# Latent attention: four modulation steps first, down projection in quarter pieces, softmax two heads deep, other modulation steps spread over the heads

## The chip, the core and the metric

One core of one Trainium2 chip runs the whole program. The metric is the device time of one launch in microseconds. The kernel before takes 2475.97 us (median of 3 runs, 2472.95 to 2480.49).

The core has TensorE (PE: matrix products out of SBUF into PSUM, which has 8 banks here), VectorE (DVE), ScalarE (ACT), GpSimd (POOL) and SyncE (SP), whose queue issues nearly all weight DMAs. Each engine works through its own program in order and waits on semaphores that the others raise.

## What is computed

Two stacks of layers in float32, on 256 tokens of width 1024. The change is in the first layer's mixer, latent attention over 256 latent and 256 context tokens; behind it follow a mixture of experts, a convolution layer, another mixture of experts, and the second stack.

```python
mod_l = (silu(c) @ w_mod[i] + b_mod[i])          # 6 * 1024 columns; mod_c the same of c_ctx
sh1, sc1, g1, sh2, sc2, g2 = split(mod_l, 6)
a_lat = rmsnorm(x, g) * (1 + sc1) + sh1          # a_ctx with the context's
...
ckv = a @ w_dkv                                  # 256 columns and 64 of a rotary key
c_kv = rmsnorm(ckv[..., :256], g_kv);  k_pe = rope(ckv[..., 256:])
k_nope, v = split((c_kv @ w_ukv).reshape(n, 8, 256))
q = (rmsnorm(a_lat @ w_dq, g_q) @ w_uq).reshape(n, 8, 192)   # 128, and 64 with rope
s = q @ concat([k_nope, k_pe]).T * scale         # 256 x 512 a head
o = softmax(s) @ v                               # 8 heads
x = x + g1 * (o @ w_o)
```

## The kernel before

`Mla` computes the latent attention; each of its methods `sync`, `tensor`, `scalar`, `vector`, `gpsimd` is one engine's program, in the order written. Everything is held with channels on the partitions.

Weights come through a ring of six slots of 128 x 4096 floats (2 MB). `Chunk.fetch` (L253) issues the DMA on SP once the slot is free; at the program's start "free" is the landing of all constants (L231). A chunk whose products run in the short float32 form takes two slots: `round_scalar` (L283) rounds the weights on ScalarE into a high part, `rest_vector` (L291) forms the low part on VectorE, and a product is then three passes, high x high, high x low, low x high (`product3`, L566). `round_piece_scalar` and `rest_piece_vector` (L298, L309) do the same for a quarter of the columns and were there already for other stages. A slot is given back by a count that TensorE raises at its last use.

The modulation has 12 steps in this layer (`Modulation`, L345), each over one 2 MB chunk of w_mod: 8 narrow products (L366), a ScalarE copy to a row (L390), four transposes on TensorE (L378, in the helper at L564), a VectorE sum (L397). Steps 0 to 3 give shift and scale for the input, the other 8 are wanted only at the attention's end and later.

Order before. SP fetches steps 0 to 2, w_dq, step 3, w_dkv, steps 4 and 5, the two w_uq, step 6, w_ukv, steps 7 to 11, the two w_o (L798 to L813), and behind it the 12 chunks of the next layer's modulation and the expert weights, the latter as half slots (L339). TensorE: mean of squares, steps 0 to 3, cq (L823, in L606 to L612, `first_linear3_tensor`), ckv and the rotary key in three tiles of 512 columns (L829, in L576), mean of cq, step 4, mean of ckv, step 5, the query products w_uq (L856, in L560) with the rotations, step 6, V (L872), then the heads.

A head h: `scores(h)` makes the keys' own part (bank "kn", L879), VectorE copies it to KN (L1065), four products give the scores in two banks (L892, L893), VectorE takes the maxima (L1072), ScalarE the exponentials with their sums (L983), VectorE divides (L1079). `values(h)` transposes the probabilities (L902), ScalarE copies them to PT (L991), four products with V give o (L908), VectorE splits it in high and low (L1084, L1086). In TensorE's order `scores(h + 1)` stands ahead of a modulation step and `values(h)`; in VectorE's order `values(h)` stands ahead of `softmax(h + 1)`. There is one pair of buffers S and one PT.

PSUM banks are handed out in turn (`Banks.next`, L203): a request waits until the bank's last reader is done; `hold` takes one out of the turn.

## Time and profile before

| | us |
|---|---|
| median of 3 runs | 2475.97 |
| span of the profiled execution | 2478.1 |
| PE busy, share of the span | 2246.1, 91% |
| DVE busy | 1011.6, 41% |
| ACT busy | 744.2, 30% |
| DMA, mean over the span | 249 GB/s |

The page's slices are 62 us each. In the first five PE's tenths are 4, 8, 8, 7, 8, from the sixth on mostly 9. The DMA rate in the first eight is 286, 257, 68, 67, 298, 412, 421, 421 GB/s: the weights of the heads were all fetched early, and the stream comes back with the output projection. The latent attention takes the first 282 us, the first mixture of experts follows.

A float32 product is recorded as two pieces, one of the short form as one. Times of the rows are read from one profiled execution; the clock that the page grants TensorE is told as a share of 2.4 GHz.

### The profile page before, as it was taken

Reading aid. Unit: us, or ns where it says so; the run is one execution under the profiler, and the core shown is the slowest. Engines: PE = TensorE matmul, PEld = TensorE weight load, DVE = VectorE, ACT = ScalarE, POOL = GpSimd, SP = SyncE. Lnnn points to the kernel's source line nnn. Section 1 sums busy time; section 2 is a strip of 40 time slices with the busy share of each in tenths; the row PEclk is TensorE's granted clock in tenths of the full one; section 3 lists DMA queues with packets and bytes.
Section 4 is the critical chain, followed back from the end, with each engine's and each line's share of the span. In section 5 each row is a group of like instructions: output and inputs, shape, how many; then the busy total and the mean of one; then the engine's idle time right before and its main releaser. Section 6 shows DMA issues by size and latency. Waiting matters only on the chain.

```text
span 2478.1 us, 31723 instructions
## 1 busy us (share of the span) xinstructions
PE 2246.1 (91%) x13638; PEld 1500.3 (61%) x13638; DVE 1011.6 (41%) x1735; ACT 744.2 (30%) x1116; POOL 244.3 (10%) x220
## 2 busy tenths in 40 slices
PE   4887899999999797999999997998999889768998
PEld 2633634444444396344444445976899889658988
DVE  2322421111111254211111115875589565546982
ACT  3122311111111242111111114865455343225542
POOL 0000000000000000000000000046136100001540
PEclk8999999999999898999999998999999989889999
DMA  8711899999999445899999984432345444203642
GB/s 286 257 68 67 298 412 421 421 421 421 413 400 401 159 169 205 323 401 399 401 398 401 403 327 139 153 120 68 128 156 177 170 155 170 102 1 104 196 161 85
DMA packets 197490, 616.89 MB, mean 249 GB/s; under 512 B 19936, under 2 KB 82528, under 8 KB 147936
## 3 DMA queue, kind: packets, MB, share of 16 engines
q1 hardware_dynamic: 189376, 610.83, 64.5%
q10 hardware_dynamic: 7968, 3.94, 0.5%
q8 instruction: 112, 1.84, 0.3%
q14 instruction: 34, 0.28, 0.0%
HBM read 613.69 MB, written 1.05 MB: 248 GB/s over the span
## 4 chain that ended last, share of the span: by engine, by line
PE 79%; DVE 9%; ACT 6%; DMA 3%; issue 1%; POOL 1%; SPq 0%; ACTq 0%; DVEq 0%; POOLq 0%
PE bank L576 25%; PE bank L1227 17%; PE bank L1236 9%; PE bank L564 5%; PE bank L1251 5%; PE bank L1200 4%; DVE ring_rounded L294 2%; ACT ring_rounded L288 2%; PE bank L560 2%; DMA ring<-in_w_mod 1%; PE bank L2868 1%; PE bank L366 1%; DMA ring<-in_moe_w_up 1%; DVE rstd L644 1%; PE bank L606 1%
## 5 line engine op out<-in xcount | busy, mean ns | idle before, releaser
L1227 PE MATMUL bank<-ring,arena 128*64 128x512 f32 x2048 | 450.6, 592 | 1.8 <-DVE arena L1586 1.6
L576 PE MATMUL bank<-normed_rounded,ring_rounded 128*128 128x256 f32 (+1 forms) x3368 | 413.2, 285 | 7.2 <-ACT normed_rounded L665 5.7
L576 PEld LDWEIGHTS bank<-normed_rounded,ring_rounded 128*128 128x128 f32 x3368 | 408.1, 190 | 9.5 <-issue 6.5
L294 DVE TENSOR_TENSOR ring_rounded<-ring,ring_rounded 128x4096 fp32r<-128x4096 f32 x69 | 307.8, 4466 | 157.3 <-ACT ring_rounded L288 157.1
L576 PE MATMUL bank<-arena_rounded,ring_rounded 128*128 128x256 f32 (+1 forms) x2416 | 313.6, 290 | 18.1 <-ACT ring_rounded L288 6.0
L1227 PEld LDWEIGHTS bank<-ring,arena 128*64 128x64 f32 x2048 | 147.5, 137 | 293.1 <-issue 291.1
L576 PEld LDWEIGHTS bank<-arena_rounded,ring_rounded 128*128 128x128 f32 x2416 | 301.5, 194 | 28.3 <-DVE ring_rounded L294 6.8
L1591 DVE TENSOR_TENSOR arena<-arena,bank 64x512 f32<-64x512 f32 x64 | 43.5, 680 | 579.4 <-ACT arena L1423 579.4
L288 ACT ACTIVATE ring_rounded<-ring 128x4096 fp32r<-128x4096 f32 x69 | 245.1, 3555 | 73.4 <-DMA ring<-in_ffn_w_down 51.1
L1236 PE MATMUL bank<-ring,arena 128*64 128x512 f32 x1024 | 233.8, 598 | 0.0
L564 PEld LDWEIGHTS bank<-mats,arena 128*128 128x128 f32 (+1 forms) x934 | 121.4, 183 | 110.1 <-issue 83.5
L564 PE MATMUL bank<-mats,arena 128*128 128x128 f32 (+1 forms) x934 | 159.4, 301 | 17.1 <-POOL arena L2346 5.3
L1423 ACT ACTIVATE arena<-bank 64x512 f32<-64x512 f32 x64 | 38.0, 594 | 406.1 <-PE bank L1227 406.1
L1437 ACT ACTIVATE arena<-bank 128x512 f32<-128x512 f32 x64 | 38.2, 597 | 366.9 <-PE bank L1236 366.9
L1236 PEld LDWEIGHTS bank<-ring,arena 128*64 128x64 f32 x1024 | 67.8, 136 | 130.5 <-issue 130.2
L1251 PE MATMUL bank<-arena 64*128 64x256 f32 x1024 | 128.3, 388 | 1.4 <-ACT arena L1437 1.4
L1580 DVE COPY arena<-bank 128x256 f32<-128x256 f32 x64 | 27.2, 425 | 248.0 <-PE bank L1251 242.8
L1200 PE MATMUL bank<-arena 128*64 128x512 f32 x512 | 122.6, 600 | 1.0 <-DVE arena L1554 1.0
L1251 PEld LDWEIGHTS bank<-arena 64*128 64x128 f32 x1024 | 93.7, 185 | 19.3 <-ACT arena L1437 3.2
L2700 DVE SCALAR_TENSOR_TENSOR arena<-arena,cols 128x256 f32<-128x256 f32 x176 | 95.3, 542 | 6.3
L2724 POOL TENSOR_TENSOR arena_rounded<-arena,arena_rounded 128x256 fp32r<-128x256 f32 x44 | 89.4, 2031 | 23.3 <-ACT arena_rounded L2649 23.3
L1200 PEld LDWEIGHTS bank<-arena 128*64 128x64 f32 x512 | 37.2, 138 | 73.6 <-issue 73.6
(257 smaller groups left out, 2103.5 us busy)
## 6 DMA issues: line engine op xcount, KB each, us to landing
ring<-in_moe_w_gate SPq DMA_DIRECT2D x128, 1024.0 KB, 8.9
ring<-in_moe_w_up SPq DMA_DIRECT2D x128, 1024.0 KB, 11.0
ring<-in_moe_w_down SPq DMA_DIRECT2D x128, 1024.0 KB, 8.1
ring<-in_w_mod SPq DMA_DIRECT2D x24, 2048.0 KB, 13.4
ring<-in_ffn_w_up SPq DMA_DIRECT2D x44, 1024.0 KB, 6.7
ring<-in_ssm_w_in SPq DMA_DIRECT2D x12, 2048.0 KB, 8.0
ring<-in_ffn_w_down SPq DMA_DIRECT2D x10, 2048.0 KB, 7.9
ring<-in_conv_w_in SPq DMA_DIRECT2D x6, 2048.0 KB, 9.2
```

The costliest lines, as they stand in the source:

```text
L288: e.activation(ring.rounded[(self.number + 1) % RING][:, 0:n].bitcast(F32R), ring.slots[self.number % RING][:, 0:n], ACT.Copy).then_inc(*s ...
L294: e.tensor_tensor(ring.rounded[slot][:, 0:n].bitcast(F32R), ring.slots[slot][:, 0:n], ring.rounded[(self.number + 1) % RING][:, 0:n], ALU. ...
L560: end = e.matmul(out, lhs(k), rhs(k), start=k == 0, stop=k == n_k - 1)
L564: return e.transpose(out, in_, self.mats[0:rows, 0, 0:rows])
L576: end = e.matmul(out, lhs.bitcast(F32R), rhs.bitcast(F32R), start=start and n == 0 and k == 0, stop=stop and n == 2 and k == n_k - 1)
L1200: end = e.matmul(bank[n * cap:(n + 1) * cap, :], self.mine[x][:, t, :], self.f[:, t, n * 512:(n + 1) * 512], start=t == 0, stop=t == self. ...
L1227: ends[i] = e.matmul(bank[rows, :], self.xt[x][:, j, n * cap:(n + 1) * cap], weights[:, j, :], start=n == 0 and j == 0, stop=n == 1 and j ...
L1236: end = e.matmul(bank[n * cap:(n + 1) * cap, :], self.ht[x][:, k, :], weights[:, i, n * 512:(n + 1) * 512], start=k == 0, stop=k == KF - 1)
L1251: end = e.matmul(self.acc(kk), self.y[x][rows, i * P:(i + 1) * P], self.back[x][rows, :], start=False, stop=last and kk % 2 == 1)
L1591: e.tensor_tensor(h, h, banks.of(key, "h", x)[0:cap, :], ALU.mult).then_inc(*dve.up(key, "h", x))
L2700: e.scalar_tensor_tensor(buf, self.PB[:, s, j, q:q + T], w3[:, q:q + 1], buf, ALU.mult, ALU.add).then_inc(*dve.up())
L2724: e.tensor_tensor(self.H_low[:, m, :].bitcast(F32R), self.H[:, m, :], self.H_high[:, m, :], ALU.subtract).then_inc(*pool.up(key, "h low", m))
```

## The change

Ring: slots that were never used need no wait, so SP issues the first weights without the constants. SP's order is modulation steps 0 to 3, w_dq, w_dkv, both w_uq, steps 4 and 5, w_ukv, steps 6 to 11, w_o.

Down projections: w_dq is rounded in four quarters, each with two tiles of the modulated input of the latent tokens, and TensorE takes them quarter by quarter; the context's half of the input is modulated afterwards. ckv and rotary key are computed for latent and context columns apart, in three banks that are held, with the mean of cq between the two. The query products wait only for the scaled cq; the mean of ckv and the rotations are put between them, steps 4 and 5 behind the two chunks.

Heads: two pairs of S, two PT and `small` for two heads. TensorE's iteration h is the keys of h + 2, the scores of h + 1, a modulation step (6 to 10 in iterations 0 to 4, 11 in iteration 6), the transposes of h, the values of h - 1. ScalarE's is the exponentials of h + 1, the step's row, the PT copies of h; w_o's two chunks are rounded behind those of heads 6 and 7. VectorE's is the sum of an earlier step, o of h - 2, the key copy of h + 2, maxima and division of h + 1; in the last iteration w_o 0's rest is first.

```diff
@@ -228,8 +228,13 @@
...
-        self.number, self.half, self.freed = 0, 0, [(self.k.constants, ("constants",))] * RING
+        self.number, self.half, self.freed = 0, 0, [None] * RING
         self.halves = {}
+
+    def wait_for(self, w, freed):
+        if freed:
+            signal, key = freed
+            w.wait_ge(*signal.at(*key))
 
     def close_halves(self):
...
@@ -254,8 +259,7 @@
...
-        signal, key = ring.freed[slot]
-        w.wait_ge(*signal.at(*key))
+        ring.wait_for(w, ring.freed[slot])
...
@@ -594,13 +596,17 @@
...
 
         pe, (high, low) = self.pe, weights
-        w.wait_ge(*chunk.ready()[0])
-        w.wait_ge(*chunk.ready()[1])
+        if not pieces:
+            w.wait_ge(*chunk.ready()[0])
+            w.wait_ge(*chunk.ready()[1])
         for i in range(n_k):
+            if pieces:
+                w.wait_ge(*self.act.at("high", chunk.name, i * 4 // n_k))
+                w.wait_ge(*self.dve.at("low", chunk.name, i * 4 // n_k))
...
@@ -752,24 +758,24 @@
...
-        self.S = [ar.take(BANK) for _ in range(2)]
+        self.S = [[ar.take(BANK) for _ in range(2)] for _ in range(2)]
...
-        self.KN, self.PT = ar.take(2, T), ar.take(4, SEQ)
+        self.KN, self.PT = ar.take(2, T), [ar.take(4, SEQ) for _ in range(2)]
...
-        self.rest = Modulation(k, 0, 4, 8, lambda at: (early if at < 7 else late)[at % 2])
+        self.rest = Modulation(k, 0, 4, 8, lambda at: (early if at < 6 else late)[at % 2])
...
@@ -796,21 +802,22 @@
...
     def sync(self, e, w):
-        for at in range(3):
+        for at in range(4):
             self.first.fetch(e, w, at)
-        self.w_dq.fetch(e, w)
-        self.first.fetch(e, w, 3)
-        self.w_dkv.fetch(e, w)
-        self.rest.fetch(e, w, 4)
-        self.rest.fetch(e, w, 5)
-        for chunk in self.w_uq:
+        for chunk in (self.w_dq, self.w_dkv, *self.w_uq):
             chunk.fetch(e, w)
-        self.rest.fetch(e, w, 6)
+        for at in (4, 5):
+            self.rest.fetch(e, w, at)
         self.w_ukv.fetch(e, w)
-        for at in range(7, 12):
+        for at in range(6, 12):
             self.rest.fetch(e, w, at)
         for chunk in self.w_o:
             chunk.fetch(e, w)
+
+    step_of = {0: 6, 1: 7, 2: 8, 3: 9, 4: 10, 6: 11}
...
@@ -820,23 +827,29 @@
...
+        def x_ready(c):
+            return lambda part, i: dve.at("mla x", "low", i, c) if part else act.at("mla x", "high", i, c)
+
+        k.first_tiles_tensor(e, w, self.w_dq, "cq", 4, self.q_parts, KD, SEQ, lambda m: dve, x_ready(0), pieces=True)
...
         for m in range(3):
-            which, cols = (0, slice(m * P, (m + 1) * P)) if m < 2 else (1, slice(0, P))
-            bank, emptied = banks.next(dve if m < 2 else act, "ckv", m)
+            _, emptied = banks.next(dve if m < 2 else act, "ckv", m)
+            banks.hold("ckv", m)
             w.wait_ge(*emptied)
-            ends = k.product3(e, w, bank[:, :], [lambda i, v=v: v[which][:, i, cols] for v in (high, low)], self.x_parts, KD,
-                              self.w_dkv.ready())
-            if m == 2:
-                ends[1].then_inc(*pe.up("free", self.w_dkv.number + 1))
-            ends[2].then_inc(*pe.up("ckv", m))
+        for c in range(2):
+            cols = self.cols_of(c)
+            for m in range(3):
+                which, at = (0, slice(m * P, (m + 1) * P)) if m < 2 else (1, slice(0, P))
+                ends = k.product3(e, w, banks.of("ckv", m)[:, cols], [lambda i, v=v: v[which][:, i, at] for v in (high, low)],
+                                  [lambda i, x=x: x(i)[:, cols] for x in self.x_parts], KD, self.w_dkv.ready(), x_ready(c))
+                if c and m == 2:
+                    ends[1].then_inc(*pe.up("free", self.w_dkv.number + 1))
+                if c:
+                    ends[2].then_inc(*pe.up("ckv", m))
+                    banks.drop("ckv", m)
+            if c == 0:
+                k.mean_tensor(e, w, "cq", self.QN, 4, SEQ, 512)
         pe.mark("free", self.w_dkv.number)
...
-        k.mean_tensor(e, w, "cq", self.QN, 4, SEQ, 512)
-        self.rest.step_tensor(e, w, 4)
-        k.mean_tensor(e, w, "ckv", self.squared, 2, T, 256)
-        self.rest.step_tensor(e, w, 5)
...
@@ -845,26 +858,33 @@
...
         for c, chunk in enumerate(self.w_uq):
...
-                w.wait_ge(*dve.at("scaled", "ckv"))
...
+                w.wait_ge(*dve.at("scaled", "cq"))
                 end = k.product(e, bank[:, 0:SEQ], lambda i: weights[:, i, t * P:(t + 1) * P], lambda i: self.CQ[:, i, :], 4)
                 end.then_inc(*pe.up("uq", c, t))
-                if t >= 4:
-                    rotate((c, t), self.QR[:, 2 * c + t - 4, :], act.at("uq", c, t))
+                if (c, t) == (0, 1):
+                    k.mean_tensor(e, w, "ckv", self.squared, 2, T, 256)
+                if (c, t) == (0, 3):
+                    rotate("k", self.raw, act.at("ckv", 2))
+                if t == 5:
+                    rotate_query(c, 4)
+                if (c, t) == (1, 0):
+                    rotate_query(0, 5)
             pe.mark("free", chunk.number)
-        w.wait_ge(*dve.at("turned", (1, 5)))
-        w.wait_ge(*act.at("uq", 1, 5))
-        self.rest.step_tensor(e, w, 6)
+            self.rest.step_tensor(e, w, 4 + c)
...
+        w.wait_ge(*dve.at("scaled", "ckv"))
...
+                if (t, n) == (0, 0):
+                    rotate_query(1, 5)
+
+        def keys(h):
...
+        def scores(h):
             kn = self.KN[:, h % 2, :]
-            outs = []
+            w.wait_ge(*dve.at("turned", (1, 5)))
             for q in range(2):
                 out, emptied = banks.next(act, "exp", h, q)
-                banks.hold("exp", h, q)
                 w.wait_ge(*emptied)
-                outs.append(out)
-            w.wait_ge(*dve.at("kn", h))
-            for q, out in enumerate(outs):
+                w.wait_ge(*dve.at("kn", h))
                 e.matmul(out[:, :], self.QN[:, h, q * P:(q + 1) * P], kn, start=True, stop=False)
                 e.matmul(out[:, :], self.QR[:, h // 2, q * P:(q + 1) * P], self.KPE[:, h % 2, :], start=False, stop=True
                          ).then_inc(*pe.up("scores", h, q))
...
-        def values(h):
+        def turns(h):
...
-                    end = k.turn(e, bank[:, i * P:(i + 1) * P], self.S[q][:, i * P:(i + 1) * P])
+                    end = k.turn(e, bank[:, i * P:(i + 1) * P], self.S[h % 2][q][:, i * P:(i + 1) * P])
...
+        def values(h):
...
             w.wait_ge(*act.at("pt", h, 1))
...
+        keys(0)
+        keys(1)
         scores(0)
         for h in range(MLA_HEADS):
-            for q in range(2):
-                banks.drop("exp", h, q)
+            if h + 2 < MLA_HEADS:
+                keys(h + 2)
             if h + 1 < MLA_HEADS:
                 scores(h + 1)
-            if h < 5:
-                self.rest.step_tensor(e, w, 7 + h, turn=True)
-            values(h)
-        self.rest.close_tensor(e, w)
+            if h in self.step_of:
+                self.rest.step_tensor(e, w, self.step_of[h])
+            turns(h)
+            if h == MLA_HEADS - 1:
+                self.rest.close_tensor(e, w)
+            if h:
+                values(h - 1)
+        values(MLA_HEADS - 1)
...
@@ -940,70 +970,81 @@
...
-        for at in range(3):
+        for at in range(4):
             self.first.step_scalar(e, w, at)
-        self.w_dq.round_scalar(e, w)
-        self.first.step_scalar(e, w, 3)
         w.wait_ge(*dve.at("mod", 0, 0))
-        k.modulated_parts_scalar(e, w, "mla x", 0, T, self.x_parts[0])
+
+        def high(i, c):
+            cols = self.cols_of(c)
...
+            e.activation(self.x_parts[0](i)[:, cols].bitcast(F32R), k.A[:, i, cols], ACT.Identity,
+                         bias=k.mod[:, 0, i, c:c + 1]).then_inc(*act.up("mla x", "high", i, c))
+        for q in range(4):
+            self.w_dq.round_piece_scalar(e, w, q)
+            for i in (2 * q, 2 * q + 1):
+                high(i, 0)
         self.w_dkv.round_scalar(e, w)
+        for i in range(KD):
+            high(i, 1)
+        for i in range(4):
+            w.wait_ge(*dve.at("cq", i))
+            e.activation(self.QN[:, i, :], self.CQ[:, i, :], ACT.Square).then_inc(*act.up("square", "cq", i))
+        k.root_scalar(e, w, "cq", SEQ)
...
+            w.wait_ge(*dve.at("ckv", i))
+            e.activation(self.squared[:, i, :], self.CKV[:, i, :], ACT.Square).then_inc(*act.up("square", "ckv", i))
...
         e.activation(self.raw, banks.of("ckv", 2)[:, :], ACT.Copy).then_inc(*act.up("ckv", 2))
...
-            e.activation(self.squared[:, i, :], self.CKV[:, i, :], ACT.Square).then_inc(*act.up("square", "ckv", i))
...
+        query(0, 0)
+        query(0, 1)
         k.root_scalar(e, w, "ckv", T, dve.at("scaled", "cq"))
-        self.rest.step_scalar(e, w, 5)
-        w.wait_ge(*pe.at("sums", "cq"))
...
         for c in range(2):
-            for t in range(6):
...
-        self.rest.step_scalar(e, w, 6)
+            for t in range(2 if c == 0 else 0, 6):
+                query(c, t)
+            self.rest.step_scalar(e, w, 4 + c)
...
+        exps(0)
         for h in range(MLA_HEADS):
-            if h < 5:
-                self.rest.step_scalar(e, w, 7 + h)
-            if h == MLA_HEADS - 1:
-                self.w_o[0].round_scalar(e, w)
-            values(h)
             if h + 1 < MLA_HEADS:
-                softmax(h + 1)
+                exps(h + 1)
+            if h in self.step_of:
+                self.rest.step_scalar(e, w, self.step_of[h])
+            turned(h)
+            if h >= MLA_HEADS - 2:
+                self.w_o[h - MLA_HEADS + 2].round_scalar(e, w)
         w.wait_ge(*pe.at("mod turn", 0, 11))
-        self.w_o[1].round_scalar(e, w)
...
@@ -1013,30 +1054,50 @@
...
-        for at in range(3):
+        for at in range(4):
...
-        self.w_dq.rest_vector(e, w)
-        self.first.step_vector(e, w, 3)
...
-        k.modulated_parts_vector(e, w, "mla x", 0, T, *self.x_parts)
...
+        for q in range(4):
+            for i in (2 * q, 2 * q + 1):
+                value(i, 0)
+            self.w_dq.rest_piece_vector(e, w, q)
+        for i in range(KD):
+            lower(i, 0)
         self.w_dkv.rest_vector(e, w)
+        for i in range(KD):
+            value(i, 1)
         for m in range(4):
             w.wait_ge(*pe.at("cq", m))
             e.tensor_copy(self.CQ[:, m, :], banks.of("cq", m)[:, 0:SEQ]).then_inc(*dve.up("cq", m))
-        for m in range(2):
-            w.wait_ge(*pe.at("ckv", m))
-            e.tensor_copy(self.CKV[:, m, :], banks.of("ckv", m)[:, :]).then_inc(*dve.up("ckv", m))
-        for buf, n_k, n, name, gain in ((self.CQ, 4, SEQ, "cq", "g_q"), (self.CKV, 2, T, "ckv", "g_kv")):
+        for i in range(KD):
+            lower(i, 1)
+
+        def scaled(buf, n_k, n, name, gain):
             k.root_vector(e, w, name, n)
...
-            if name == "ckv":
-                self.rest.step_vector(e, w, 4)
+        scaled(self.CQ, 4, SEQ, "cq", "g_q")
+        for m in range(2):
+            w.wait_ge(*pe.at("ckv", m))
+            e.tensor_copy(self.CKV[:, m, :], banks.of("ckv", m)[:, :]).then_inc(*dve.up("ckv", m))
+        scaled(self.CKV, 2, T, "ckv", "g_kv")
...
@@ -1087,21 +1150,25 @@
...
-        self.rest.step_vector(e, w, 5)
+        last = MLA_HEADS - 1
         key_part(0)
+        key_part(1)
         softmax(0)
         for h in range(MLA_HEADS):
-            if h + 1 < MLA_HEADS:
-                key_part(h + 1)
-            if h < 5:
-                self.rest.step_vector(e, w, 6 + h)
-            if h == MLA_HEADS - 1:
+            if h == last:
                 self.w_o[0].rest_vector(e, w)
-            values(h)
+            if h in (1, 2, 3, 4, 5, 7):
+                self.rest.step_vector(e, w, 4 + h if h < 6 else 10)
+            if 2 <= h:
+                values(h - 2)
+            if h + 2 < MLA_HEADS:
+                key_part(h + 2)
             if h + 1 < MLA_HEADS:
                 softmax(h + 1)
         self.rest.step_vector(e, w, 11)
         self.rest.close_vector(e, w)
+        values(last - 1)
+        values(last)
         self.w_o[1].rest_vector(e, w)
         for m in range(KD):
```

## Rows read from the trace of the kernel before

**Rows 1.** Chain that ended last, first 150 us: start us, length us, what.
```profile
11.68 0.37 SPq L264
...
47.64 4.33 DVE ring_rounded L294
52.54 6.43 DVE normed L682 x16
...
68.60 16.80 PE bank L576 x72
...
99.19 10.51 PE bank L560 x40
...
113.89 8.65 PE bank L560 x40
...
130.59 15.47 PE bank L560 x36
```

**Rows 2.** The same chain over one head.
```profile
175.86 2.01 PE bank L908 x8
...
182.32 1.10 PE bank L892 x2
...
185.99 1.85 PE bank L366 x16
187.84 1.04 PE bank L564 x8
...
190.04 2.01 PE bank L908 x8
```

**Rows 3.** The same chain from the last head into the experts.
```profile
254.87 3.78 PE bank L908 x8
...
259.51 22.65 PE bank L576 x192
...
331.61 22.69 DMA ring<-in_moe_w_up
...
366.99 6.87 PE bank L1227 x32
...
382.76 6.87 PE bank L1227 x32
```

**Rows 4.** Instructions in order of time: start, length, instruction [idle before <-releaser].
```profile
37.25 3.62 ACT L288 ACTIVATE ring_rounded<-ring 128x4096 fp32r<-128x4096 f32 x1 [1.08 <-DMA ring<-in_mla_w_dq]
42.72 3.64 PE L366 MATMUL bank<-ring,silu_cond 128*32 128x512 f32 x16 [6.17 <-DMA ring<-in_w_mod]
```

**Rows 5.** By stretch: busy PE, PEld, DVE, ACT, POOL; granted clock, DMA share, GB/s.
```profile
6.00:12.00 6.00, 0.00 (x0) 0.00 (x0) 0.00 (x0) 0.22 (x1) 0.29 (x1) 1.00 0.84 303
12.00:17.00 5.00, 2.86 (x4) 1.33 (x5) 0.00 (x0) 3.64 (x7) 0.67 (x1) 1.00 0.83 276
...
22.00:27.00 5.00, 3.17 (x26) 0.69 (x28) 3.35 (x1) 1.19 (x2) 0.00 (x0) 1.00 1.05 387
...
52.00:58.00 6.00, 3.83 (x18) 3.86 (x19) 5.90 (x17) 4.88 (x13) 0.00 (x0) 0.50 0.08 27
...
180.00:200.00 20.00, 14.19 (x56) 6.78 (x56) 6.00 (x15) 3.99 (x11) 0.00 (x0) 1.00 0.00 1
...
370.00:400.00 30.00, 30.00 (x158) 12.83 (x156) 5.28 (x14) 4.34 (x8) 0.00 (x0) 1.00 1.01 421
```

**Rows 6.** SP's queue: waits (us, times, longest), issue of w_o, its landing.
```profile
SPq L264 <- PE bank L560: 105.2, 1, 105.2
...
SPq L264 <- DMA rows<-in_rows: 9.8, 1, 9.8
...
235.65 0.99 SPq L264 DMA_DIRECT2D ring<-in_mla_w_o  x2
...
DMA to landing us min/median/max: 7.8/10.3/12.8
```

**Rows 7.** Waits from 146 to 260 us: who, for whom, us in total, times.
```profile
PE bank L892 <- DVE arena L1065: 18.9, 8, 2.7
```

93 lines of the change are left out of this document (51 added, 42 removed).

## The prediction

> **What bounds the kernel now.** First the page's slices: TensorE is busy for most of the span, but its holes are in the first eighth, which is the latent attention. So I read the chain of waits over that stretch, then the stage behind it. The stage that is edited ends where the last product of the attention ends, 259.51 + 22.65 = 282.16 us [rows 3]. What comes after is unchanged, so the question is whether a microsecond won before 282.16 arrives at the end. Behind the attention the chain runs through DMAs of weights once (22.69 us for the first expert pieces) and then through TensorE alone: the experts follow each other every 382.76 - 366.99 = 15.77 us [rows 3], TensorE busy in all 30 us of a stretch of 30 [rows 5]. The DMA stream of that stage can only restart when the first half of the output projection frees its ring slot, about half of 22.65 us before 282.16, so it is tied to the attention's end and moves with it. I take what is won in the attention at full worth.
>
> In the attention three things cost. (1) The start: the SP queue issues no weight before 11.68 us [rows 1], since it waits 9.8 us for the constants [rows 6]; then modulation steps end at 42.72 + 3.64 and VectorE rounds w_dq for 4.33 us before it may modulate, at 52.54 [rows 1, 4]. (2) From the end of the down projections at 68.60 + 16.80 = 85.40 to the first query product at 99.19 there are 13.79 us of norm latency [rows 1]. (3) The heads: one head's loop is 190.04 - 175.86 = 14.18 us [rows 2], in which TensorE works and then waits for VectorE and ScalarE; in 20 us of heads it is busy for 14.19 [rows 5], and the wait for the key copy alone is 18.9 us over the 8 heads [rows 7].
>
> **The change, part by part**, on the profiled execution's own clock (span 2478.1).
>
> *Start.* SP no longer waits for the constants. How much DMA time was idle? From 6 to 12 us the engines moved 303 GB/s, from 12 to 17 us 276, where 387 is the full rate [rows 5]: 6 x 84 + 5 x 111 = 1059 KB, at 387 GB/s 2.7 us. The rest of those 10 us was used by the constants themselves, so the stream comes only 2.7 us earlier, not 10. The order adds more: the weights landed in the order mod 0, 1, 2, w_dq, mod 3, each 2.1 MB in 42.72 - 37.25, about 5.4 us [rows 4]. With mod 3 ahead of w_dq it lands at 42.72 - 2.7 - 5.4 = 34.6 and w_dq at 40.0. Step 3 then costs what it did, 3.64 us plus turn and closing; from 42.72 to the modulation before were 9.82 us, of which 4.33 rounding w_dq [rows 1, 4], so 34.6 + 5.5 + 0.8 = 40.9. The 0.8 is the two turns that I let end late. Won: 52.54 - 40.9 = 11.6 us. The first products need w_dq's first quarter (3.62/4 = 0.9 us on ScalarE, two values at 6.43/16 = 0.4, 4.33/4 = 1.1 on VectorE): they begin at 43.0, 2.1 us after the modulation's start; before they began about 1.6 us after it. A quarter then costs VectorE 0.8 + 1.1 = 1.9 us, 7.8 for four; TensorE needs 16 products a quarter, 1.9 us at 0.118 each and 3.4 at half clock, so it sets the pace. Before, 52.54 to 68.60 were 16.1 us; now 2.1 + 13.1 = 15.2 (64 products, the first 3.9 us at half clock, then 32 at 0.118), to 56.1. 0.118 is 22.65/192 [rows 3].
>
> *Down projection of the key side in two column halves.* 144 products of 256 columns at 0.118 = 17.0 us for 72 at 16.80/72 = 0.233 [rows 1]: +0.2. The mean of cq goes between them: 8 pieces at 8.65/40 = 0.216 are 1.7 us [rows 1], work that stood behind before. VectorE in its queue does the 8 lower parts (to 48.7), w_dkv's rest (3072 columns where 4.33 us are for 4096: 3.3, to 55.3 by the landing and rounding ahead of it), 8 values, 4 copies, 8 lowers (to 63), root and scaling of cq (to 70.4). Needed: w_dkv's rest by 58, the second half's parts by 64.6, scaled cq by the end, 56.1 + 17.0 + 1.7 = 74.8. All in time, the closest by about 2 us; w_dkv's small pieces could cost that. End 74.8 for 85.40.
>
> *Query products.* They wait only for scaled cq, so the 13.79 us of latency go. The norm of ckv, a part of them, lies beside 12 x 8 x 0.216 = 20.8 us of products. Counted on TensorE to the first head: 20.8, five rotations 2.2, ckv mean 1.7, steps 4 and 5 with a turn 2 x 1.85 + 0.46 = 4.2 [rows 2], V 32 x 15.47/36 = 13.75 [rows 1], 1.0 for small waits: 43.7. First head 118.5. Before it stood at 130.59 + 13.75 = 144.3 [rows 1], so 25.8 us are won up to here. The queue: w_uq no longer stands behind the modulation weights, and w_ukv waits for the end of the down projections, 74.8, and lands some 8 us later [rows 6], 20 us before V.
>
> *Heads.* Scores, probabilities and transposes of head h run in other iterations: products of keys h+2, scores h+1, a modulation step, transposes h, values h-1. TensorE's work is keys 4 x 0.43 = 1.72, scores 8 x 0.43 = 3.44, step 1.85, 12 transposes at 1.04/8 = 1.5, values 8 x 0.216 = 1.73: 10.2 us, where the loop took 14.18 [rows 2]. What else could end last: in the 20 us of heads VectorE is busy for 6.00 and ScalarE for 3.99 [rows 5], too little to bound. Their in-order queues: VectorE's read of o(h-2) waits for the last product of the iteration before, and key copy h+2 and maxima h+1 are queued behind; that is ready as the iteration starts, and the maxima come 1.7 + 1.7 us later, so nothing is late. The banks: an iteration with a step takes 8, so each is asked for again one iteration later, when its reader is done. Up to keys(7), which frees w_ukv: 8 keys 13.8, 6 scores 20.6, 5 steps with turns 11.8, 5 x 8 transposes 5.0, 4 values 6.9, and 1.0 for waits: 59.0, at 177.5.
>
> *The end of the heads.* Here SP's queue matters: mod 11 now waits for w_ukv's slot, and w_o stands behind it. SP waited 105.2 us for that slot before, until 235.65, and two 2 MB chunks landed 7.8 and 12.8 us after their issue [rows 6]. So mod 11 lands at +7.8, w_o 0 at +13, w_o 1 at +18.4. Step 11 is wanted at +9.9: covered. ScalarE rounds w_o 0 after the copies of head 6: +14.2 to +17.8; VectorE its rest to +22.4 [rows 1, 4]. In its queue behind it stands step 10's read, and the bank of the last values product is the one that this read empties: values(7) cannot start before +22.7. After 3.8 us without work it runs at the lower clock, as it did before (3.78 us [rows 3]), to +26.5; then 22.65 + 0.2. End at +49.4: 226.9 us. This is the price of the order; before, the same stretch took 282.16 - 235.65 = 46.5 us [rows 3, 6].
>
> **Sum**: 282.2 - 226.9 = 55.3, as 11.6 + 0.9 (start, cq) - 1.9 (halves and mean) + 15.2 (latency and query stage) + 29.5 (heads). The profile is 2.1 us above the runs' median of 2475.97, and its difference counts against that median: 2476.0 - 55.3 = 2420.7, so 2421.
>
> **A rule that speaks against the heads.** At 14.19 busy of 20 us the granted clock in the heads is 1.00, the level of 2.4 GHz; it was 0.50, that of 1.2 GHz, from 52 to 58 us, where TensorE came back from waiting for the modulation [rows 5]. The Trainium skill (TensorE: Matmul & The Clock Gate, "A second HAM failure mode: psum-queue depth-cycling") says that cycling through banks every iteration leaves short idles after which the clock swings between its levels. The new loop cycles through all 8 banks. By rows it is rival C.
>
> **Rivals.**
> A. The overlap isn't had: some wait in the in-order queues (a bank, the read of o before the key copy) keeps the old period of about 14 us for the heads. For it: VectorE's queue does hold old reads ahead of new maxima. Against it: each dependency above has 2 us or more. It costs 7 x 4.0 = 28: 2449. Half of it, 2435.
> B. The constants come late, because the weights are queued beside them. From the rows: if they come only with mod 0 or mod 1 (18.4 or 23.8 us, for 11.7), the mean, 8.6 us long, ends at 29 to 35 and four steps of 1.9 to 2.1 at 38 to 43, for 39 now: 0 to +4 us, 2425. The Trainium skill (DMA: Bandwidth & Descriptors, "Queues, rings and completion order") says that a DMA's semaphore write lands only after every earlier write of that DMA engine, across its queues. By that rule this happens; no row before shows it.
> C. The slower one: the clock. If the heads ran at 1.2 GHz, TensorE's 77 us of work in them (8 x 7.9 for keys, scores, transposes and values, 6 x 2.35 for steps) become 154: 2421 + 77 = 2498. It turns the sign from 55 of the 77 us at the lower level. Against it: clock 1.00 at less load [rows 5].
> D. The stream behind doesn't move along, or the change's waits cancel it: 2470.
>
> **How the numbers follow.** Forecast case (with B's small cost and errors of about 8 us in the start and the heads' end) 0.76, between 2408 and 2433. A, whole or half, 0.17. D 0.04, C 0.02, anything faster than 2408 0.01. To hold 8 in 10 the range takes in the forecast case and half of A: 2409 to 2440. A difference under 0.3% (7 us) can't be told from none. Faster 0.95, same 0.03, slower 0.02.
>
> **What would show it.** After: modulation from about 41 us; the first query product directly behind the last down product, near 75; head loops of 10 to 10.5 us with TensorE over 90% busy and clock 1.00; keys(7) near 177.5; a hole of about 4 us ahead of the last values product, behind VectorE's rounding of w_o; the output product ending near 227; experts still every 15.77 us. Wrong if the heads' period is above 12, if TensorE waits on w_mod or w_ukv anywhere in them, if the clock falls in them, or if the DMA wait ahead of the experts grows.

## The result, and the profile after

The changed kernel takes 2421.40 us (median of 4 runs, 2414.76 to 2423.29) beside 2477.89 for the kernel before (median of 4, 2472.95 to 2480.49). The ratio is 0.9768, 95% interval 0.9748 to 0.9788. The forecast was 2421, in a range of 2409 to 2440. The profiled execution has a span of 2418.3 us for 2478.1.

Page of the kernel after, its span and the engines' busy time:

```profile
span 2418.3 us, 31875 instructions
...
PE 2230.9 (92%) x13710; PEld 1499.3 (62%) x13710; DVE 1012.0 (42%) x1738; ACT 745.9 (31%) x1119; POOL 244.7 (10%) x220
```

The share of TensorE moves from 91% to 92% only: the time came out of one stage, and only that stage's rows show it. The start, in order of time (start, length, instruction, and in brackets the idle time ahead of it with what ended it):

```profile
1.87 18.15 SPq L268 DMA_DIRECT2D ring<-in_w_mod  x4
...
11.95 0.22 ACT L735 ACTIVATE silu_cond<-cols 128x16 f32<-128x16 f32 x1 [8.10 <-DMA rows<-in_rows]
...
34.65 3.62 PE L368 MATMUL bank<-ring,silu_cond 128*32 128x512 f32 x16 [2.92 <-DMA ring<-in_w_mod]
```

SP issues weights from 1.87 us on (11.68 before [rows 1]); the constants are there at 11.95 all the same; step 3's chunk lands at 34.65. Next the chain of waits, from the modulation to the heads:

```profile
40.33 0.88 DVE normed L1066 x2
41.21 1.23 DVE ring_rounded L314
...
53.06 3.80 PE bank L618 x32
...
67.05 8.47 PE bank L578 x72
75.51 3.45 PE bank L562 x16
...
106.32 15.45 PE bank L562 x36
...
154.05 1.72 PE bank L562 x4
155.77 0.86 PE bank L913 x2
...
159.20 1.85 PE bank L368 x16
161.06 1.46 PE bank L566 x12
162.52 1.73 PE bank L931 x8
164.25 1.72 PE bank L562 x4
```

The down projections end at 75.52 and the first query product (L562) starts there: the 13.79 us between [rows 1] are gone. One head is 164.25 - 154.05 = 10.20 us for 14.18 [rows 2], and it consists of TensorE's own pieces with nothing between. The stretches say the same (columns as in [rows 5]):

```profile
118.00:176.00 58.00, 58.00 (x254) 29.29 (x253) 24.73 (x56) 19.54 (x41) 0.00 (x0) 1.00 0.03 12
```

TensorE is busy for 58.00 of 58.00 us at a granted clock of 1.00, the level of 2.4 GHz; before it was 14.19 of 20 [rows 5]. The end of the heads, on SP's queue and in the chain:

```profile
176.60 3.87 SPq L268 DMA_DIRECT2D ring<-in_mla_w_o  x2
```

```profile
188.54 1.08 ACT arena L1032 x2
189.63 3.52 ACT ring_rounded L291
...
193.17 4.43 DVE ring_rounded L297
...
197.75 3.02 PE bank L931 x8
200.76 23.19 PE bank L578 x192
```

And who waited for whom there (us in total, times, longest):

```profile
PE bank L931 <- DVE mod L399: 4.0, 1, 4.0
```

This is the hole that the prediction put behind VectorE's rounding of w_o 0: the last values product waits 4.0 us for the bank that step 10's read (L399) empties. The attention ends at 223.95 for 282.16 [rows 3], 58.2 us earlier. The experts behind it still follow each other every 324.48 - 308.71 = 15.77 us [rows 3].

```profile
308.71 6.87 PE bank L1294 x32
...
324.48 5.57 PE bank L1294 x25
```

### The profile page after: what moved, and what is told of

It reads as the page before. It is cut to its first block, busy times and chain, and to the rows that moved or that the text cites. A ratio compares the mean times of both kernels' runs of the same rounds, so it can differ in the third digit from the quotient of the medians.

```text
span 2418.3 us, 31875 instructions
## 1 busy us (share of the span) xinstructions
PE 2230.9 (92%) x13710; PEld 1499.3 (62%) x13710; DVE 1012.0 (42%) x1738; ACT 745.9 (31%) x1119; POOL 244.7 (10%) x220
## 4 chain that ended last, share of the span: by engine, by line
PE 81%; DVE 8%; ACT 6%; DMA 2%; issue 1%; POOL 1%; SPq 1%; ACTq 0%; DVEq 0%; POOLq 0%
PE bank L578 25%; PE bank L1294 18%; PE bank L1303 9%; PE bank L566 5%; PE bank L1318 5%; PE bank L1267 5%; ACT ring_rounded L291 2%; DVE ring_rounded L297 2%; PE bank L562 2%; DMA ring<-in_w_mod 1%; PE bank L368 1%; PE bank L2935 1%; PE bank L612 1%; PE bank L613 1%; PE bank L2913 1%
## 5 line engine op out<-in xcount | busy, mean ns | idle before, releaser
L578 PE MATMUL bank<-normed_rounded,ring_rounded 128*128 128x256 f32 x3392 | 413.2, 283 | 7.2 <-ACT normed_rounded L671 5.7
L297 DVE TENSOR_TENSOR ring_rounded<-ring,ring_rounded 128x4096 fp32r<-128x4096 f32 (+2 forms) x68 | 303.4, 4466 | 156.7 <-ACT ring_rounded L291 156.4
L578 PE MATMUL bank<-arena_rounded,ring_rounded 128*128 128x256 f32 x2464 | 317.0, 289 | 18.7 <-ACT ring_rounded L291 6.1
L578 PEld LDWEIGHTS bank<-arena_rounded,ring_rounded 128*128 128x128 f32 x2464 | 306.5, 195 | 27.2 <-ACT ring_rounded L291 6.7
L1658 DVE TENSOR_TENSOR arena<-arena,bank 64x512 f32<-64x512 f32 x64 | 43.5, 680 | 578.7 <-ACT arena L1490 578.7
L291 ACT ACTIVATE ring_rounded<-ring 128x4096 fp32r<-128x4096 f32 (+2 forms) x68 | 241.4, 3553 | 70.7 <-DMA ring<-in_ffn_w_down 50.9
L566 PE MATMUL bank<-mats,arena 128*128 128x128 f32 (+1 forms) x934 | 156.8, 298 | 13.5 <-POOL arena L2413 4.7
L1504 ACT ACTIVATE arena<-bank 128x512 f32<-128x512 f32 x64 | 38.2, 597 | 366.8 <-PE bank L1303 366.8
```

What stands on the lines that cost most here:

```text
L291: e.activation(ring.rounded[(self.number + 1) % RING][:, 0:n].bitcast(F32R), ring.slots[self.number % RING][:, 0:n], ACT.Copy).then_inc(*s ...
L297: e.tensor_tensor(ring.rounded[slot][:, 0:n].bitcast(F32R), ring.slots[slot][:, 0:n], ring.rounded[(self.number + 1) % RING][:, 0:n], ALU. ...
L566: return e.transpose(out, in_, self.mats[0:rows, 0, 0:rows])
L578: end = e.matmul(out, lhs.bitcast(F32R), rhs.bitcast(F32R), start=start and n == 0 and k == 0, stop=stop and n == 2 and k == n_k - 1)
L1658: e.tensor_tensor(h, h, banks.of(key, "h", x)[0:cap, :], ALU.mult).then_inc(*dve.up(key, "h", x))
```

## The experiments

Marks that I compare: first keys of head 0; the end of keys(7), which frees w_ukv for w_o; the attention's last product. Of the changed kernel: 118.33, 176.16, 223.95. keys(h) is the product that makes head h's own key part. All marks are from one profiled execution each; the last experiment shows how far they scatter by themselves. The experiments ran on three chips, and the kernel before beside them on each: the front alone, the heads alone, the wait for the constants and w_dq whole on one; the keys twice, the copy thrice, the rest later and the quarters of w_o 0 on a second; the rest on a third. The chip of the changed kernel's first profile is not on record. So the ratios compare within a chip; the marks set beside the first profile may not.

### The front alone

Everything up to V as changed, the heads, softmax and the order of their queues as before (one S, one PT; `values(h)` ahead of `softmax(h + 1)`). w_ukv is fetched ahead of step 7, and six steps, 6 to 11, are worked in the heads, where the kernel before has five. The cut below is shortened.

```
-        for h in ...: keys(h + 2); scores(h + 1); step; turns(h); values(h - 1)
+        for h in ...: scores(h + 1); step; values(h)        # of the kernel before
```

> The changed start, down projections and query stage, with the heads of the kernel before (one pair S, one PT; steps 6 to 11 in heads 0 to 5, w_ukv fetched ahead of step 7). Theory: the front is worth 25.8 us by itself, so the first head's keys begin near 118.4 us and the heads keep a period of 14.2 us; the time is 2478 - 26 + 1 = 2453 us. Rival (the gain of the front is given back, since the modulation weights or w_ukv come too late for the heads): the period is above 14.5 or TensorE waits for w_mod or w_ukv there, and the time is above 2460.

Median 2455.41, ratio 0.9913 (0.9886 to 0.9941). Its chain:

```profile
105.55 13.75 PE bank L562 x32
...
157.25 1.10 PE bank L914 x2
...
171.43 1.10 PE bank L914 x2
...
234.91 22.59 PE bank L578 x192
```

The 32 pieces are 28 of V and the 4 of keys(0), so V is done and the heads begin at 117.58 (118.33 in the changed kernel), 26.8 us earlier than before. The period of a head is 171.43 - 157.25 = 14.18 as before where the clock holds. The attention ends at 257.50: the front alone is worth 24.7 us. The period doesn't always hold: from 141.37 to 157.25 it is 15.88, and so it is once more from 185.61 on; in the kernel before it is 15.87 once, and the row there is

```profile
211.00:216.00 5.00, 5.00 (x11) 1.73 (x9) 0.00 (x0) 0.00 (x0) 0.00 (x0) 0.66 0.00 0
```

The granted clock is 0.66 in these 5 us, so TensorE is for a part of them at the level of 1.2 GHz; in the 67 us before, it had been busy for 50.51.

### The heads alone

The reverse: the kernel before with the heads' two buffers, split loops and new order.

> The front of the kernel before (SP's order too), with the new heads and two pairs of S and PT (steps 7 to 11 in heads 0 to 4). Theory: TensorE sets the pace, period 10.2 us, keys(7) end 57.8 us after the heads' start near 144.3. Here step 11 doesn't stand behind keys(7) and w_o 0 lands 5 us earlier after it, so the last product ends some 46 us after keys(7), near 248: 34 us won, 2444 us. Rival (the two parts only help together, since the heads' weights are early in one order alone): period above 11, or less than 28 us won, over 2450.

Median 2437.71, ratio 0.9848 (0.9819 to 0.9876); the attention ends at 244.62, 37.5 us earlier than before.

```profile
178.00 1.72 PE bank L560 x4
...
188.19 1.72 PE bank L560 x4
...
222.59 22.03 PE bank L576 x185
```

The period is 10.19. The end comes 3.4 us earlier than expected: 2 us of it stand already at the first keys, 1.6 of them since the first 40 pieces of the query products take 8.89 us for 10.51 [rows 1], and the rest is a shorter tail. The two halves add up to 24.7 + 37.5 = 62.2, where both together give 58.2. The 4.0 us that are missing are the net of three stages:

| us from mark to mark | before | front alone | heads alone | both |
|---|---|---|---|---|
| start to first keys | 144.3 | 117.6 | 142.3 | 118.3 |
| first keys to the end of keys(7) | 91.3 | 95.4 | 57.8 | 57.8 |
| keys(7) to the attention's end | 46.5 | 44.6 | 44.5 | 47.8 |

In the tail each half alone gains 2.0 us, and both together lose 1.3. In the heads-only kernel step 11's chunk is long fetched when keys(7) frees w_ukv, and w_o 0 is the first to go out; in the changed kernel step 11's goes ahead of it, so that ScalarE's rounding starts 13.5 us after keys(7) and not 12.0 (at 212.08), and a step's read stands behind VectorE's rest. Ahead of the heads the halves add up to 2.9 us more than both give. Against these 5.3 and 2.9 us stand 4.1 that the front alone loses in its heads, which work one step more and meet the lower clock twice (all rounded).

### SP waits for the constants again

```
     def sync(self, e, w):
+        w.wait_ge(*self.k.constants.at("constants"))
         for at in range(4):
```

> The changed kernel with SP waiting for the constants ahead of its first weight, as before. Theory: the constants used most of those 10 us of DMA time themselves, so mod 3 lands 2.7 us later (37.3 for 34.65 us) and everything behind it moves by 2.7 us, to about 2424 us. Rival (the SP wait was the whole delay): 10 us later, mod 3 at 44.7 and 2431 us. Second rival (the steps were covered by the mean): no move.

The first issue is back at 11.71, yet step 3's chunk lands only 37.10 - 34.65 = 2.45 us later:

```profile
37.10 1.92 PE L368 MATMUL bank<-ring,silu_cond 128*32 128x512 f32 x16 [1.58 <-DMA ring<-in_w_mod]
```

This mark lies at 34.41 to 34.97 in the nine profiles with the changed kernel's first fetches, so the price is 2.45 within some 0.3, beside the 2.7 that the idle DMA time of [rows 5] gave. It doesn't arrive whole: at the end of keys(7), 177.47, 1.3 us are left, because TensorE's first products run at the lower clock for 3.1 us here and for 5.7 in the changed kernel. The attention ends at 226.59, 2.6 later, but 1.3 of that is the tail's (values(7) takes 3.78 for 3.02, the output product 23.62 for 23.19), which this edit doesn't touch. The median is 2422.28 (ratio 0.9778, 0.9752 to 0.9803), which alone could not have shown any of it.

### w_dq ahead of step 3

The changed kernel with one move in SP's list: w_dq goes out before step 3's chunk.

```
-        for at in range(4):
+        for at in range(3):
             self.first.fetch(e, w, at)
-        for chunk in (self.w_dq, self.w_dkv, *self.w_uq):
+        self.w_dq.fetch(e, w)
+        self.first.fetch(e, w, 3)
+        for chunk in (self.w_dkv, *self.w_uq):
```

> The changed kernel with one move on SyncE's list: the four chunks of w_dq are fetched ahead of modulation step 3, as in the kernel before, and every engine still works the four steps first. It prices the order of the fetches by itself. Theory of the prediction: the start is bound by the transfers in their order, so step 3 lands w_dq's transfer time later, 5.4 us (from 34.65 to about 40.1), the modulation starts that much later, and w_dq's earlier landing gives nothing back, since its pieces wait for the same step; attention's last product ends about 5.4 us later, near 229.4, and the time is about 2427. Rival: w_dq's rounding moves under step 3's landing and gives most of it back: attention ends within 1.5 us of the changed kernel's 223.95.

```profile
39.93 3.64 PE bank L368 x16
...
46.16 0.88 DVE normed L1068 x2
...
206.28 22.57 PE bank L578 x192
```

Step 3 lands at 39.93, 5.3 us later, the modulation starts at 46.16, 5.8 later, and the attention ends at 228.85, 4.9 later. Median 2426.92, ratio 0.9786 (0.9755 to 0.9816). Against the changed kernel's second profile, taken on the same chip (last experiment), keys(7) is 3.7 and the attention's end 3.4 us later: there w_dq's own landing, at 41.58, holds up the first quarter, where here nothing waits for it. So the order of two fetches is worth 3.4 to 4.9 us of the front's 25, and the rival, which allowed 1.5, is refuted. w_dq is one chunk; the expectation calls it four.

### w_dq rounded whole

```
-        for q in range(4):
-            self.w_dq.round_piece_scalar(e, w, q)
-            for i in (2 * q, 2 * q + 1):
+        self.w_dq.round_scalar(e, w)
+        for i in range(KD):
                 high(i, 0)
```

and likewise on VectorE and in TensorE's waits.

> The changed kernel with w_dq rounded in one piece again, ahead of the modulation, and the products waiting for all of it. Theory: ScalarE's 3.6 and VectorE's 4.4 us stand one behind the other from 40.1 us, so the first product begins near 49 instead of 42.7, and TensorE, which set the pace in the quarters, makes up at most 1 us of it: the query stage starts 5 to 6 us later, 2427 us. Rival (the quarters bring nothing, since VectorE sets the pace of the first pass either way): within 1 us of 2421.

The first product starts at 49.12 for 42.70, keys(7) ends at 181.78, 5.6 us later, and the attention at 229.73, 5.8 later. Yet the span is 2418.6, that of the changed kernel (2418.3), and the median 2424.37 (ratio 0.9796, 0.9771 to 0.982): the execution made up in its late stages what this one lost in the attention. That was unexpected, and the last section is about it.

### What sets the pace of the heads

Once TensorE is given more to do in each head, once VectorE.

```
             w.wait_ge(*emptied)
+            k.product(e, bank[:, :], lambda i: w_heads[:, i, h, 0, :], lambda i: self.CKV[:, i, :], 2)
             end = k.product(...)                       # the key product, made twice
```

> The changed kernel, each head's key product computed twice in its bank (TensorE +1.72 us a head, nothing else longer). Theory (TensorE sets the pace of the heads): keys(7) and all behind it come 8 x 1.72 = 13.8 us later, period 11.9 us, 2435 us. Rival (the chain over maxima, exponentials, division sets it, and TensorE has slack): less than 5 us more.

```
+            for n in range(2):
+                e.tensor_copy(self.KN[:, h % 2, :], banks.of("kn", h)[:, :]).then_inc(*dve.up())
+                w.wait_ge(*dve.now())
             e.tensor_copy(self.KN[:, h % 2, :], banks.of("kn", h)[:, :]).then_inc(*dve.up("kn", h))
```

> The changed kernel, each head's key copy done three times on VectorE (+2 x 0.7 = 1.4 us a head ahead of the maxima, 11 us over the heads). Theory (VectorE's queue has over 2 us of slack in an iteration): the period stays 10.2 us and the last product ends within 1 us of 223.95. Rival (rival A of the prediction: old reads and copies ahead of the new maxima are near to setting the pace): period up by 1 us or more, over 8 us in all.

With the keys made twice the chain has this:

```profile
151.76 3.43 PE bank L562 x8
...
163.67 3.43 PE bank L562 x8
...
215.93 22.92 PE bank L578 x192
```

The period is 163.67 - 151.76 = 11.91, that is 1.72 more, all of the added 4 pieces of 0.43; keys(7) ends at 190.92, 14.8 later, of which 13.8 are the products and 1.0 the start; the attention ends at 238.85 (median 2433.97, ratio 0.9817, 0.9781 to 0.9853). With the copy made thrice the stretch from 128 to 170 us reads

```profile
128.00:170.00 42.00, 42.00 (x192) 21.41 (x191) 25.06 (x54) 13.62 (x31) 0.00 (x0) 1.00 0.00 1
```

VectorE is busy for 25.06 us of 42, for 18.05 in the same stretch of the changed kernel, and the period stays 10.19 (165.97 - 155.78). The attention ends at 226.93, later by 3.0, where the expectation had 1 us: 0.9 of it is the start, 0.9 a wait ahead of the first scores, where three copies of keys(0) stand with no other work of TensorE's before them, and 1.2 the tail, which the edit doesn't touch. The median is 2423.59 (0.9782, 0.9745 to 0.9819). So TensorE sets the pace and not VectorE, and the copy that was waited for 18.9 us before [rows 7] has 1.4 us of room in each head. ScalarE, busy for 13.74 of the 42 us, was not slowed down in a run.

### The hole ahead of the last values product

w_o 0's rest is put behind step 10's read and `values(5)` in VectorE's queue.

```
-            if h == last:
-                self.w_o[0].rest_vector(e, w)
             if h in (1, 2, 3, 4, 5, 7): ...
             if 2 <= h:
                 values(h - 2)
+            if h == last:
+                self.w_o[0].rest_vector(e, w)
```

> The changed kernel; in VectorE's last iteration step 10's sum and the reading of o 5 stand ahead of w_o 0's rest instead of behind it. Theory (the 4.0 us hole ahead of the last values product is the bank that this sum empties): the hole shrinks to under 1 us, and since o 7 is then read right behind the rest, the output product ends about 2.6 us earlier, near 221.3 us. Rival (the hole is ScalarE's copy of head 7 behind w_o 0's rounding): the hole stays above 3 us and nothing moves.

The wait for L399 is gone, and the first output product now waits for VectorE's reading of o instead (both from its chain):

```profile
194.70 4.42 DVE ring_rounded L297
...
200.49 0.34 DVE arena_rounded L1147
...
200.88 22.06 PE bank L578 x185
```

From the end of keys(7), 177.61, to the end of attention, 222.94, are 45.3 us for 47.8: the hole cost 2.5, close to the expected 2.6 and not its whole 4.0, because the rounding itself is still late (47.8 is the shortest such stretch; without an edit it goes up to 49.1, see the last experiment). Counted from the execution's start the end comes only 1.0 us earlier, since keys(7) is 1.45 later here. Median 2416.95, ratio 0.9759 (0.9726 to 0.9792).

### w_o 0 rounded earlier, in quarters

Step 6 is fetched ahead of w_ukv, so that step 11's fetch no longer stands between keys(7) and w_o 0; the steps are worked at heads 0 to 5 in a row; ScalarE rounds w_o 0 in quarters behind head 5's turns; VectorE does two quarters ahead of its reads of values(6) and (7) and two behind.

```
-    step_of = {0: 6, 1: 7, 2: 8, 3: 9, 4: 10, 6: 11}
+    step_of = {h: 6 + h for h in range(6)}
...
+            if h == 5:
+                for q in range(4):
+                    self.w_o[0].round_piece_scalar(e, w, q)
...
```

> The changed kernel with another end of the heads: w_ukv fetched ahead of step 7, so steps 6 to 11 go with heads 0 to 5 and w_o is the first fetch behind keys(7); w_o 0 is rounded in quarters on ScalarE behind head 5's copies and VectorE's quarters are put around the last three reads of o. Theory: keys(7) ends where it did, w_o 0 is there 7.8 us later, no rounding stands between head 7's transposes and its values; the output product ends 43.3 us after keys(7) for 47.8, near 219.5 us: 4.5 us less than the changed kernel, about 2417 us. Rival (VectorE's reads of o set the end, whatever the rounding): under 1.5 us won.

On ScalarE and TensorE, in order of time:

```profile
184.78 3.90 ACT L306 ACTIVATE ring_rounded<-ring 128x1024 fp32r<-128x1024 f32 x4 [0.42 <-DMA ring<-in_mla_w_o]
```

```profile
199.44 2.15 PE L578 MATMUL bank<-arena_rounded,ring_rounded 128*128 128x256 f32 x16 [1.36 <-DVE ring_rounded L314]
```

w_o 0 is there at 184.78, 7.9 us after keys(7) for 13.5. keys(7) ends at 176.92 and the attention at 220.41: 43.5 us for 47.8. What is left is a stall of 1.36 us ahead of 199.44, for VectorE's last two quarters. Median 2414.30, ratio 0.974 (0.9711 to 0.9769).

The same kernel, with TensorE taking w_o 0's 64 products that need only high parts of the weights first, in four banks, and the 32 with low parts behind them:

```
+        for t in range(4):          # high x high, high x low
+            for b in range(2):
+                for i in range(KD): e.matmul(banks.of("mla y", t)..., high[:, i, cols[t]], parts[b](i), ...)
+        w.wait_ge(*chunk.ready()[1])
+        for t in range(4):          # low x high
+            for i in range(KD): e.matmul(..., low[:, i, cols[t]], parts[0](i), ...)
```

> The kernel of the tail experiment (w_o 0 rounded in quarters from head 5 on, modulation steps at six heads in a row, VectorE's rests in quarters) with one thing more on TensorE: of w_o 0's 96 products the 64 that need only the high parts of the weights run first, over four banks, and the 32 with the low parts after them, so that VectorE's last two quarters lie under products and not ahead of the first. Theory: what is left between keys(7) and the end of attention is products, the turns, values(6) and (7) and the last head's chain; attention's last product ends about 41 us after keys(7), near 217.9, some 2.5 us less than without the move, and the time is near 2412. Rival: the first product of w_o waits for the reading of head 7's output all the same, or starts at the lower clock, and the end stays within 1 us of 220.4.

```profile
196.61 7.58 PE bank L970 x64
204.19 3.79 PE bank L976 x32
207.99 11.35 PE bank L578 x96
```

The stall is gone. From keys(7), at 177.33, are 42.0 us, 1.5 less than without the move, where 2.5 were expected: the stall that it removes was 1.36, as the row above shows. By the attention's end alone, 219.34, the rival's bound of 1 us around 220.4 is just left; the start of this execution was 0.4 later. Median 2417.19 (2402.77 to 2423.59), ratio 0.9739 (0.9705 to 0.9773). By their marks the last two kernels end the attention 3.5 and 4.6 us earlier than the changed kernel's first profile, and their tails, 43.5 and 42.0 us, lie below the 47.8 to 49.1 of all seven profiles in which the tail is unedited. Their medians are lower too, by 7 and 4 us, but the intervals of the ratios overlap its own.

### The changed kernel once more

> The changed kernel itself once more, with nothing edited: it shows how far marks and spans scatter by themselves. Expected: attention's last product within 1.5 us of 223.95, the fetch of conv_w_in 556.3 to 556.9 us behind it as in every kernel so far, and the rest of the execution different by up to some 5 us from the 2194.4 us of the first profile, together with the granted clock of the late stage (0.89 to 0.94 so far); the median within 0.3% of 2421.4. If the rest comes out within 1 us of 2194.4 instead, the differences seen in the other kernels' late stages are made by the edits and not by the execution.

Nothing edited: median 2420.97 (2412.95 to 2423.28), ratio 0.9751 (0.9722 to 0.978). Marks: keys(7) at 177.26, attention's end at 225.43, later by 1.1 and 1.5. The 1.1 come from the start: here ScalarE waits for w_dq's landing until 41.58, where in the first profile it began at 40.12, released by the modulation. Both rows of this execution, of step 3's product and of w_dq's first quarter:

```profile
41.58 1.06 ACT L306 ACTIVATE ring_rounded<-ring 128x1024 fp32r<-128x1024 f32 x1 [3.51 <-DMA ring<-in_mla_w_dq]
```

```profile
34.60 2.83 PE L368 MATMUL bank<-ring,silu_cond 128*32 128x512 f32 x16 [2.91 <-DMA ring<-in_w_mod]
```

The rest of the execution is 2421.4 - 225.4 = 2196.0 us for 2194.4. So a mark in the attention is good to about 1.5 us. The tail, keys(7) to the end, is 48.2 for 47.8 here, and over the seven profiles that leave it unedited it is 47.8 to 49.1: such an interval is good to about 1.3 us. One that TensorE fills at the clock 1.00, like the period of a head, repeats to 0.01. What follows the attention scatters by more, as the last section shows.

## Why the prediction was right, step by step

**The start.** Step 3's landing was put at 34.6 (34.65 measured), the modulation's start at 40.9 (40.33), the end of cq at 56.1 (56.86), the end of the down projections at 74.8 (75.52). Its parts were tried one by one: the missing wait was priced at 2.7 and is 2.45; the order of the fetches at 5.4, which moves step 3 by 5.3 and the end by 3.4 or 4.9, by the profile that it is set against; the quarters by the expectation at 5 to 6, which are 5.8. That w_dq would land at 40.0, just under the need, held in one profile of the changed kernel and not in the other (41.58). One term was too small: TensorE was put at the lower clock for the first 3.9 us of the cq products, and its pieces take 0.21 for 5.7 us, from 42.70 to 48.37 (granted clock 0.59 from 40.0 to 48.4), which makes cq end 0.8 late though its first product was 0.3 early. In the profiles of the front alone and of the wait for the constants the same spell is 4.2 and 3.1 us: this is part of the start's scatter. The price of the halves was counted right: 67.05 + 8.47 - 56.86 = 18.7 for 17.0 + 1.7.

**Rival B**, constants late by up to 4 us: the cast of the conditioning, which waits for them, runs at 11.95 with three chunks started beside them (issues from 1.87, 5.37 and 9.47 us on). Before, the same cast ran at 11.69. That is 0.3 us. The rule of the Trainium skill that stood behind it (DMA: Bandwidth & Descriptors, "Queues, rings and completion order") gave no delay beyond that here. Whether it would bite where more of the chunks has been started before the constants, no run shows.

**The latency.** 15.2 us were counted for it and the query stage; measured, from the end of the down projections to the first keys, 118.33 - 75.52 = 42.8 for 144.3 - 85.40 = 58.9: 16.1. The 1.0 us for small waits that were not there is most of the difference. First keys at 118.3 for a forecast of 118.5 is so good because this and the late end of the down projections, 0.7, cancel.

**The heads.** 10.2 us a head forecast from TensorE's pieces, 10.20 measured; keys(7) at 177.5 and 176.16. That TensorE and nothing else sets it was an argument from busy shares in the prediction; the doubled key product (+1.72 of 1.72) and the tripled copy (+0.00) show that it is TensorE and not VectorE, and with 58.00 of 58.00 us busy TensorE has no wait left that ScalarE could end. The 1.3 us that keys(7) is early are the 1.0 for waits that did not come and 0.2 from the start. Rival A, a wait that keeps the old period, is refuted, and so is C: the clock stays at 1.00 through all of the heads. The prediction argued against C that the old heads, with more idle time, had 1.00 as well; that was read from 20 us, and in 211 to 216 us of the kernel before it is 0.66. The change thus took short spells at the lower clock away, each some 1.7 us of one head. The Trainium skill's rule on depth-cycling (TensorE: Matmul & The Clock Gate, "A second HAM failure mode: psum-queue depth-cycling") is about short idles; the loop uses all eight banks in each head, and with 58.00 of 58.00 us busy it has none.

**The tail.** This was the least certain term, 49.4 us, and measured 47.8. The mechanism is the one described: w_o issued at the end of keys(7), ScalarE's rounding, VectorE's rest, step 10's read behind it, and values(7) behind that. Two terms were too large: the read was put at +22.7 and the product started at +21.6 (ScalarE began at +13.5, not +14.2, and VectorE's rest ended at +21.4, not +22.4), and the product takes 3.02 us, where I took 3.78 from the kernel before. The mechanism of this piece was not as in the prediction, which had the clock fall in the idle time: it is 1.00 up to 198.5 us, while the product already runs, and 0.51 from 198.5 to 202.0. Before, it was 0.50 already when the product started.

```profile
197.75:198.50 0.75, 0.75 (x4) 0.67 (x4) 0.72 (x3) 0.75 (x1) 0.00 (x0) 1.00 1.05 388
198.50:202.00 3.50, 3.50 (x13) 3.06 (x12) 2.40 (x8) 2.88 (x3) 0.00 (x0) 0.51 1.05 386
```

So the output product's first pieces ran at the lower clock too, and it took 23.19 where 22.65 + 0.2 were counted. That leaves -1.1 - 0.8 + 0.3 = -1.6.

**From the mark to the time.** I took what is won before the attention's end at full worth. Between the end of attention and the first fetch of the convolution layer's weights (its rows before and after below) lie 556.5 us before, 556.4 after, and 556.3 to 556.9 in the eleven profiles of the experiments with ends from 219 to 258: the first mixture of experts shifts as one piece, so rival D is refuted in every one of them. The attention's end moved by 58.2, the forecast's by 55.3 (1.3 at keys(7), 1.6 in the tail), and the medians by 56.5. The forecast time, 2420.7, is thus closer to the median, 2421.4, than its own mark was to the trace's, and that is luck: the base it was taken from, 2475.97, was 1.9 below the 2477.89 that the change is measured against, and the gain 1.2 below the measured one; neither scatter was priced.

```profile
838.64 61.09 SPq L264 DMA_DIRECT2D ring<-in_conv_w_in  x6
```

```profile
780.35 61.14 SPq L268 DMA_DIRECT2D ring<-in_conv_w_in  x6
```

**What stays open.** When w_dq lands goes by the chip, or by the time at which that chip's kernels ran: 39.89 and 40.14 us in the profiles of the first chip, 41.32 to 41.82 on the second, 41.47 and 41.58 on the third, with the same first fetches; why, no run shows. The first keys follow: 117.6 in the front alone on the first chip, 119.1 to 119.8 on the other two. Step 3's product takes 1.92, 2.83 or 3.62 us at the same start (34.60 to 34.67): the granted clock is 1.00 around the first and 0.59 from 34.0 to 38.2 around the last, with 2.9 us of idle time ahead of each, and what decides between them was not tried. The front's largest term, the latency behind the down projections, was tried only with the whole front, and in the heads no run tries the second buffers without the new order; which of them the shorter period needs is not shown.

## What to carry to other kernels

Where an in-order loop ties several engines together, sum the bottleneck engine's own pieces. In this loop each hand-over could be moved a whole iteration away and the buffers doubled, and that sum, written down before the result, was the new period within 0.1 us. Such a change moves the bound to the loop's end, where the work that used to be hidden (here one weight's rounding ahead of the output product) stands bare: 3.5 to 4.6 us more were had from there by the marks. And judge edits of a few microseconds by the interval between marks around the stage they touch, beside a second profile of the unedited kernel on the same chip, and not by spans.

## What the runs showed of the hardware that I had not expected

The time behind the attention, in which no experiment edits anything, isn't constant: span less attention's end is 2194.4 in the changed kernel, and over the others from 2186.9 to 2199.6. It goes with the granted clock of the late stages. Busy times and clock of 230 us there, in the changed kernel and then in the one with the rest later:

```profile
2084.00:2314.00 230.00, 188.94 (x1385) 180.74 (x1385) 159.07 (x240) 93.99 (x141) 60.56 (x39) 0.91 0.30 95
```

```profile
2083.00:2313.00 230.00, 190.58 (x1443) 182.96 (x1444) 165.71 (x247) 96.52 (x142) 64.75 (x41) 0.93 0.30 97
```

Where this clock is 0.93 or 0.94 (five kernels) the rest takes 2186.9 to 2193.6 us, where it is 0.89 to 0.91 (eight) 2194.4 to 2199.6. That this much comes without any edit is shown by the changed kernel's own runs, span against mean granted clock of the whole execution: 2412.9, 2412.7 and 2411.2 at 0.964, and the other six 2418.3 to 2421.4 at 0.959 to 0.962. Whether the clock makes the time, or a wait that comes first makes both, these rows don't show. Nine runs of one and the same kernel spread over 10 us in this way, 0.4% of the time, which is more than most of the edits tried here are worth.
